# Gated group norm of a hybrid decoder layer: one 1/512 matrix spreads the means, GpSimd takes the root over all tokens

## The chip, the core and the metric

The kernel runs on one core of a Trainium2 chip. The metric is device time in microseconds (us), median of several runs. The engines are TensorE (PE in the rows; its weight loads are PEld), VectorE (DVE), ScalarE (ACT), GpSimd (POOL) and SyncE (SP), which issues the loads.

## The reference, cut to what matters

The layer has a Mamba-2 branch (SSD) and an attention branch, then a gated FFN. The change touches only the gated norm at the end of the SSD branch:

```python
# y: (1, 256 tokens, 4096 channels), 8 groups of 512 channels
y = y + d_skip[:, None] * xh
y = y.reshape(b, s, 8, 512) * silu(z).reshape(b, s, 8, 512)
y = y * rsqrt(mean(y * y, axis=-1, keepdims=True) + 1e-5)   # one mean per token and group
y = y.reshape(b, s, 4096) * ssm_norm_w
y_ssm = y @ w_ssm_out
```

The input projection that feeds it is `u @ w_in`, with u of 256 tokens by 2048 channels, in float32.

## The kernel before

Activations lie with channels on the 128 partitions and tokens along the free dimension. For one group of 512 channels `y` is thus a tile of 128 partitions by 4 blocks by 256 tokens, and the norm needs a sum over the 4 blocks and over the partitions, and then the same factor on every partition for each token.

Weights are streamed in units of 512 KB through four slots. For each unit ScalarE writes `hi`, the rounded half (`hi_of`, L466), VectorE writes `lo = raw - hi` (`lo_of`, L901, a subtraction of 128x1024 with both inputs in SBUF), and TensorE multiplies both halves with the activations (`columns`, L1485 with 512 columns and L1487 with 256, 8 pairs in a unit; `rows`, L1470 to L1472). A unit's products wait for its `lo` (semaphore `lo_ready`). `hi` of a unit waits until the products of the unit four before have used the slot.

Every engine's program is written out by hand in its own order. The projection of the SSD branch runs in 8 groups of 20 units (`group`), then 16 units of queries and gates (`X_UN`), then blocks of 8 units per attention head group (`Q_UN`). While the units of group g run, the SSD work and norm of group g-1 are done beside them, at fixed units: `ssd_side` on VectorE and ScalarE, `ssd_after` on TensorE. The norm of one group before the change, with its unit numbers in VectorE's order:

- unit 12: `ssd_skip` writes `y`; unit 13: `ssd_gate`; ScalarE then squares into `ysq`.
- unit 17: `ssd_sum` (L1157), one reduction over the 4 blocks into `ysum`.
- TensorE, after its unit 16: `mean_y` (L1690), for each half of the tokens one product with `ysum` as weights and one column of 1/512, so that the means lie with tokens on the partitions, 128x2.
- unit 19: `ssd_mean` (L1162) adds eps. GpSimd: `y_root` (L424), a power of -0.5 over 128x2.
- next group, unit 0: `ssd_spread` (L1166) copies the roots to `rb`, 128x256. TensorE, after its unit 0: `turn_root` (L1697) transposes `rb` so that each token's root lies on every partition of PSUM.
- next group, unit 3: `ssd_scale` (L1171), four operations that read `y` and the roots in PSUM.

The last group's norm does the same in the 16 units of `X_UN` and, for the scaling, at unit 3 of the first block of `Q_UN`. GpSimd's other work in that region is the copies of keys and values (L431, L434) and the scaling of queries (L440).

Of the kernel before, what the change touches and what calls it, by code (L numbers as in the profile page):

```python
# [105 lines left out]
def build(nc, x, params, w_in, w_ssm, w_attn, w_o, w_fi, w_fo, fnorm, out):  # L106
# [5 lines left out]
    with ExitStack() as ctx:  # L112
# [19 lines left out]
        inv_w, top = place("inv_w", [P, TT], top)  # L132
# [36 lines left out]
        ysum, a = place("ysum", [P, SEQ], a)  # L169
# [9 lines left out]
        ysq, a = place("ysq", [P, 4, SEQ], region + 80 * KB)  # L179
        ktok, a = place("ktok", [P, TT, KVH, 2, HD], region + 80 * KB)  # L180
# [73 lines left out]
        y_summed, y_meaned, y_mean_ready, y_rstd = sem("y_summed"), sem("y_meaned"), sem("y_mean_ready"), sem("y_rstd")  # L254
        y_spread, y_rt, y_kept = sem("y_spread"), sem("y_rt"), sem("y_kept")
# [127 lines left out]
        def _(po):  # L383
# [5 lines left out]
            po.memset(inv_w[:], 1.0 / GW)  # L389
# [56 lines left out]
            q_scaled_in(1, B, J_X + 1)  # L446
            with po.Fori(1, KVH) as h:
# [449 lines left out]
        def _(ve):  # L897
# [257 lines left out]
            def ssd_sum(k):  # L1155
                ve.wait_ge(y_squared, k + 1)
                ve.tensor_reduce(ysum[:, :, None], ysq[:].rearrange("p i n -> p n i"), op=ALU.add, axis=AX.X) \  # L1157
                    .then_inc(y_summed, 1)

            def ssd_mean(k):  # L1160
                ve.wait_ge(y_meaned, k + 1)
                ve.tensor_scalar(ssum[:], ps[:, M + 3, SEQ:SEQ + TT], EPS, None, ALU.add).then_inc(y_mean_ready, 1)  # L1162

            def ssd_spread(k):
                ve.wait_ge(y_rstd, k + 1)
                ve.tensor_copy(rb[:], rstd[:, :, None].to_broadcast([P, TT, P])).then_inc(y_spread, 1)  # L1166

            def ssd_scale(k):
                ve.wait_ge(y_rt, k + 1)
                for i in range(4):  # L1170
                    last = ve.scalar_tensor_tensor(out=acts[:, ds(k * 4 + i, 1), :].rearrange("p a n -> p (a n)"),  # L1171
                                                   in0=y[:, i, :], scalar=pcol("ssm_norm", k * 4 + i),
                                                   in1=ps[:, M + 3, 0:SEQ], op0=ALU.mult, op1=ALU.mult)
                last.then_inc(y_kept, 1)

            STEPS = dict(inputs=5, low=8, high=9, skip=12, gate=13, sum=17, mean=19)

            def ssd_side(k, u, at=STEPS, older=True):
# [19 lines left out]
                if u == at["mean"]:  # L1198
                    ssd_mean(k)
# [714 lines left out]
```

## Time and profile before

| what | value |
|---|---|
| median of 3 runs | 1923.75 us (1923.6 to 1923.87) |
| the profiled execution's own time | 1923.14 us |
| its span, first to last instruction | 1921.4 us |
| PE busy | 1910.4 us, 99% |
| DVE busy | 1308.0 us, 68% |
| ACT busy | 1083.7 us, 56% |
| POOL busy | 38.0 us, 2% |
| granted TensorE clock, mean | 0.999 |

The busy times are of one profiled execution. PE busy counts modelled ends of pipelined products, so what one product costs is read from the distance between starts. The median of the runs is 0.6 us above the profiled execution's own time.

### The profile page before, as it was taken

To read this page: it belongs to the slowest core of one execution; us is meant where nothing else is said; L and a number is where in the kernel's file an instruction comes from. 1 tells how busy PE (TensorE), PEld (TensorE's weight loads), DVE (VectorE), ACT (ScalarE), POOL (GpSimd) and SP (SyncE) were. 2 spreads that over 40 slices of the span, in tenths; PEclk is the share of its full clock that TensorE was granted. 3 is DMA by queue.
4 is the path that set the end of the run, shared out by engine and by line. 5 is a ranking of instruction groups with operands and counts; after the bars stand their busy time and mean duration, and the time that the engine had idled before them with its cause. 6 is when DMAs were issued, how large, how long until landed. Compare 5 with 4: busy or idle time off the path is not lost.

```text
span 1921.4 us, 28874 instructions
## 1 busy us (share of the span) xinstructions
PE 1910.4 (99%) x10205; PEld 1624.1 (85%) x10205; DVE 1308.0 (68%) x1634; ACT 1083.7 (56%) x1478; POOL 38.0 (2%) x79
## 2 busy tenths in 40 slices
PE   9999999999999999999999999999999999999998
PEld 7888888888888878888888888888888888888886
DVE  6787788777878874645544778666666766645444
ACT  6566765677657764444344445666666666534443
POOL 1000000000010100000000000000000000000000
PEclk9999999999999999999999999999999999999999
DMA  7666666656654446666666576666666666566564
GB/s 248 198 187 186 187 195 190 190 170 196 206 160 137 131 127 213 196 189 195 196 190 194 186 240 207 188 186 195 188 192 190 186 186 193 188 198 195 192 194 143
DMA packets 294902, 361.52 MB, mean 188 GB/s; under 512 B 13168, under 2 KB 218032, under 8 KB 293424
## 3 DMA queue, kind: packets, MB, share of 16 engines
q1 hardware_dynamic: 294832, 360.59, 61.2%
q8 instruction: 43, 0.70, 0.1%
q14 instruction: 27, 0.22, 0.0%
HBM read 358.38 MB, written 2.16 MB: 188 GB/s over the span
## 4 chain that ended last, share of the span: by engine, by line
PE 99%; issue 0%; DMA 0%; DVE 0%; ACT 0%; SPq 0%; POOLq 0%; POOL 0%; DVEq 0%; ACTq 0%
PE ps L1485 36%; PE ps L1487 18%; PE ps L1470 14%; PE ps L1471 14%; PE ps L1472 14%; PE ps L1683 1%; PE ps L1611 1%; PE ps L1624 1%; PE ps L1635 0%; PE ps L1684 0%; PE ps L1672 0%; PE ps L1527 0%; PE ps L1562 0%; PE ps L1636 0%; PE ps L1668 0%
## 5 line engine op out<-in xcount | busy, mean ns | idle before, releaser
L901 DVE TENSOR_TENSOR lo<-raw,hi 128x1024 fp32r<-128x1024 f32 x652 | 796.2, 1227 | 467.6 <-ACT hi L466 461.6
L1485 PE MATMUL ps<-uHL,hi 128*128 128x512 f32 x2944 | 1035.3, 396 | 0.0
L466 ACT ACTIVATE hi<-raw 128x1024 fp32r<-128x1024 f32 x652 | 682.8, 1055 | 511.3 <-PE ps L1472 379.7
L1487 PE MATMUL ps<-uHL,lo 128*128 128x256 f32 x2944 | 823.9, 280 | 0.0
L1485 PEld LDWEIGHTS ps<-uHL,hi 128*128 128x128 f32 x2944 | 551.7, 187 | 130.5 <-issue 5.4
L1487 PEld LDWEIGHTS ps<-uHL,lo 128*128 128x128 f32 x2944 | 555.9, 189 | 0.0
L1472 PE MATMUL ps<-hi,aL 128*128 128x512 f32 x384 | 149.5, 389 | 0.0
L1472 PE MATMUL ps<-hi,hL 128*128 128x512 f32 x352 | 136.9, 389 | 0.0
L1471 PE MATMUL ps<-lo,hH 128*128 128x512 f32 x352 | 136.9, 389 | 0.0
L1470 PE MATMUL ps<-hi,hH 128*128 128x512 f32 x352 | 136.9, 389 | 0.0
L476 ACT ACTIVATE hb<-ps 128x512 f32<-128x512 f32 x92 | 54.8, 595 | 121.5 <-PE ps L1487 121.5
L1470 PE MATMUL ps<-hi,uHL 128*128 128x512 f32 x288 | 113.5, 394 | 0.9 <-DVE lo L908 0.9
L1472 PE MATMUL ps<-hi,uHL 128*128 128x512 f32 x288 | 112.2, 390 | 0.0
L1471 PE MATMUL ps<-lo,uHL 128*128 128x512 f32 x288 | 112.2, 389 | 0.0
L1470 PE MATMUL ps<-hi,aHs 128*128 128x512 f32 x256 | 100.9, 394 | 0.0
L1471 PE MATMUL ps<-lo,aHs 128*128 128x512 f32 x256 | 99.7, 389 | 0.0
L1472 PEld LDWEIGHTS ps<-hi,aL 128*128 128x128 f32 x384 | 72.1, 188 | 15.1
L1470 PEld LDWEIGHTS ps<-hi,hH 128*128 128x128 f32 x352 | 66.1, 188 | 13.8
L1471 PEld LDWEIGHTS ps<-lo,hH 128*128 128x128 f32 x352 | 66.1, 188 | 13.8
L1472 PEld LDWEIGHTS ps<-hi,hL 128*128 128x128 f32 x352 | 66.1, 188 | 13.5
L1092 DVE SCALAR_TENSOR_TENSOR cv<-cs,par,cv 128x253 f32<-128x253 f32 (+1 forms) x144 | 63.3, 481 | 14.2 <-ACT cv L580 7.0
L1470 PEld LDWEIGHTS ps<-hi,uHL 128*128 128x128 f32 x288 | 54.1, 188 | 12.1 <-DVE lo L908 1.1
(204 smaller groups left out, 1695.3 us busy)
## 6 DMA issues: line engine op xcount, KB each, us to landing
raw<-w_in SPq DMA_DIRECT2D x261, 512.0 KB, 4.2
raw<-w_ffn_in SPq DMA_DIRECT2D x176, 512.0 KB, 3.8
raw<-w_ffn_out SPq DMA_DIRECT2D x88, 512.0 KB, 4.4
raw<-w_ssm_out SPq DMA_DIRECT2D x64, 512.0 KB, 4.2
raw<-w_attn_out SPq DMA_DIRECT2D x32, 512.0 KB, 4.4
raw<-w_o SPq DMA_DIRECT2D x32, 512.0 KB, 4.5
rows_b<-cum_rows SPq DMA_DIRECT2D x8, 1024.0 KB, 6.7
x_tok<-x SPq DMA_DIRECT2D x8, 256.0 KB, 5.4
```

Of the source, the lines that this page charges most:

```text
L466: act.activation(hi[:, s % SLOTS, :], raw[:, s % SLOTS, :], ACT.Copy).then_inc(hi_ready, 1)
L476: act.activation(hb[:], ps[:, pair:pair + 2, SEQ:2 * SEQ], ACT.Copy).then_inc(half_kept, 1)
L901: ve.tensor_tensor(lo[:, s % SLOTS, :], raw[:, s % SLOTS, :], hi[:, s % SLOTS, :].bitcast(F32), ALU.subtract).then_inc(lo_ready, 1)
L1092: last = ve.scalar_tensor_tensor(out=cv[:, slot, sh:SEQ], in0=cs[:, i, 0:SEQ - sh], scalar=pcol("conv_w", ch * TAPS + tap), in1=cv[:, slot ...
L1470: pe.matmul(out, w[0], x[0], start=start, stop=False)
L1471: pe.matmul(out, w[0], x[1], start=False, stop=False)
L1472: return pe.matmul(out, w[1], x[0], start=False, stop=stop)
L1485: pe.matmul(ps[:, pair + c, :], w_hi, uHL[:, kk].rearrange("p a n -> p (a n)"), start=kk == 0, stop=False)
L1487: last = pe.matmul(ps[:, pair + c, 0:SEQ], w_lo, uHL[:, kk, 0, :], start=False, stop=kk == k - 1)
L1611: last = pe.matmul(ps[:, M + j, cols], qT[r, i, blk * P:(blk + 1) * P], kcur[r, keys], start=True, stop=True)
L1624: last = pe.transpose(ps[:, M + 2 + o // 512, o % 512:o % 512 + P], lg[:, i, j, c * P:(c + 1) * P], ident[:])
L1683: pe.matmul(out, xd[:, 0, c], dec[:, h, 0:2, :].rearrange("p c n -> p (c n)"), start=True, stop=False)
```

## The change

The sum over the four blocks is made by two additions (128x512, 128x256). The sum is then split into a rounded half `ymH` and a rest `ymL`, and TensorE multiplies a full 128x128 matrix of 1/512 (`mean_w`) with each, 256 columns, both into the same PSUM region. Every partition then has the mean of every token. VectorE adds eps and writes all of it to SBUF (`y_rt`, 128x256), GpSimd takes the power in place over 128x256, and `ssd_scale` reads `y_rt` at unit 10 instead of 3 (last group: unit 7 instead of 3). `ssd_spread` and `turn_root` are gone. The last group's root stands behind the first copies and query scalings on GpSimd. The first transposes of attention probabilities wait for `y_mean_ready` instead of `y_kept`.

```diff
@@ gpsimd
-            po.memset(inv_w[:], 1.0 / GW)
+            po.memset(mean_w[:].bitcast(F32), 1.0 / GW)
@@
             def y_root(k):
                 po.wait_ge(y_mean_ready, k + 1)
-                po.tensor_tensor(rstd[:], ssum[:], neghalf[:], ALU.pow).then_inc(y_rstd, 1)
-
-            with po.Fori(0, G) as g:
+                po.tensor_tensor(y_rt[:], y_rt[:], neghalf[:, 0:1].to_broadcast([P, SEQ]), ALU.pow).then_inc(y_rooted, 1)
+
+            with po.Fori(0, G - 1) as g:
                 y_root(g)
@@
             q_scaled_in(0, A, J_X + 1)
             q_scaled_in(1, B, J_X + 1)
+            y_root(G - 1)
@@ vector
             def ssd_sum(k):
                 ve.wait_ge(y_squared, k + 1)
-                ve.tensor_reduce(ysum[:, :, None], ysq[:].rearrange("p i n -> p n i"), op=ALU.add, axis=AX.X) \
-                    .then_inc(y_summed, 1)
-
-            def ssd_mean(k):
+                ve.tensor_tensor(ysq[:, 0:2, :], ysq[:, 0:2, :], ysq[:, 2:4, :], ALU.add)
+                ve.drain()
+                ve.tensor_tensor(ysq[:, 2, :], ysq[:, 0, :], ysq[:, 1, :], ALU.add)
+                ve.drain()
+                ve.tensor_copy(ymH[:], ysq[:, 2, :])
+                ve.drain()
+                ve.tensor_tensor(ymL[:], ysq[:, 2, :], ymH[:].bitcast(F32), ALU.subtract).then_inc(y_summed, 1)
+
+            def ssd_root(k):
                 ve.wait_ge(y_meaned, k + 1)
-                ve.tensor_scalar(ssum[:], ps[:, M + 3, SEQ:SEQ + TT], EPS, None, ALU.add).then_inc(y_mean_ready, 1)
-
-            def ssd_spread(k):
-                ve.wait_ge(y_rstd, k + 1)
-                ve.tensor_copy(rb[:], rstd[:, :, None].to_broadcast([P, TT, P])).then_inc(y_spread, 1)
+                ve.tensor_scalar(y_rt[:], ps[:, M + 3, 0:SEQ], EPS, None, ALU.add).then_inc(y_mean_ready, 1)
 
             def ssd_scale(k):
-                ve.wait_ge(y_rt, k + 1)
+                ve.wait_ge(y_rooted, k + 1)
@@
-                                                   in1=ps[:, M + 3, 0:SEQ], op0=ALU.mult, op1=ALU.mult)
+                                                   in1=y_rt[:], op0=ALU.mult, op1=ALU.mult)
@@
-            STEPS = dict(inputs=5, low=8, high=9, skip=12, gate=13, sum=17, mean=19)
+            STEPS = dict(scale=10, inputs=5, low=8, high=9, skip=12, gate=13, sum=17, mean=19)
@@
-            LAST_STEPS = dict(inputs=5, low=7, high=8, skip=11, gate=12, sum=13, mean=15)
+            LAST_STEPS = dict(scale=9, inputs=5, low=7, high=8, skip=11, gate=12, sum=13, mean=15)
@@
-                if u == 3:
+                if u == 7:
                     ssd_scale(G - 1)
@@ tensor
-                    pe.wait_ge(y_kept, G)
+                    pe.wait_ge(y_mean_ready, G)
@@
             def mean_y(k):
                 pe.wait_ge(y_summed, k + 1)
-                for t in range(TT):
-                    last = pe.matmul(ps[:, M + 3, SEQ + t:SEQ + t + 1], ysum[:, t * P:(t + 1) * P], inv_w[:, 0:1],
-                                     start=True, stop=True)
-                last.then_inc(y_meaned, 1)
-
-            def turn_root(k):
-                pe.wait_ge(y_spread, k + 1)
-                for t in range(TT):
-                    last = pe.transpose(ps[:, M + 3, t * P:(t + 1) * P], rb[:, t, :], ident[:])
-                last.then_inc(y_rt, 1)
+                pe.matmul(ps[:, M + 3, 0:SEQ], mean_w[:], ymH[:], start=True, stop=False)
+                pe.matmul(ps[:, M + 3, 0:SEQ], mean_w[:], ymL[:], start=False, stop=True).then_inc(y_meaned, 1)
```

How the change moves VectorE's instructions is seen at the end of one group and the start of the next (the branch at L1203, in the new code L1206, is the loop's head; `lo` is the subtraction of a unit). Before:

```order
L901 TENSOR_TENSOR lo<-raw,hi 128x1024 [waits hi_ready] x2
L1157 TENSOR_REDUCE ysum<-ysq 128x256 [waits y_squared]
L901 TENSOR_TENSOR lo<-raw,hi 128x1024 [waits hi_ready]
L951 TENSOR_TENSOR szb<-ps,hb 128x512 [waits second_half_kept]
L957 TENSOR_TENSOR szb<-szb,rt 128x512
L901 TENSOR_TENSOR lo<-raw,hi 128x1024 [waits hi_ready]
L1162 TENSOR_SCALAR ssum<-ps 128x2 [waits y_meaned]
L1203 UNCONDITIONAL_BRANCH
L1203 ISA
L901 TENSOR_TENSOR lo<-raw,hi 128x1024 [waits hi_ready]
L1165 REGISTER_ALU
L1166 COPY rb<-rstd 128x256 [waits y_rstd]
```

After, at the same place:

```order
L1160 TENSOR_TENSOR ysq<-ysq 128x512 [waits y_squared]
L1162 TENSOR_TENSOR ysq<-ysq 128x256
L1164 CAST ymH<-ysq 128x256
L1166 TENSOR_TENSOR ymL<-ysq,ymH 128x256
L904 TENSOR_TENSOR lo<-raw,hi 128x1024 [waits hi_ready]
L954 TENSOR_TENSOR szb<-ps,hb 128x512 [waits second_half_kept]
L960 TENSOR_TENSOR szb<-szb,rt 128x512
L904 TENSOR_TENSOR lo<-raw,hi 128x1024 [waits hi_ready]
L1170 TENSOR_SCALAR y_rt<-ps 128x256 [waits y_meaned]
L1206 UNCONDITIONAL_BRANCH
L1206 ISA
L904 TENSOR_TENSOR lo<-raw,hi 128x1024 [waits hi_ready]
```

One reduction has become four operations, the addition of eps covers 256 columns, and the copy that waited for GpSimd's root is gone. Directly behind the addition the `lo` of the next unit follows, in both.

GpSimd's queue from the loop over the groups to the loop over the head groups, before:

```order
L424 TENSOR_TENSOR rstd<-ssum,neghalf 128x2 [waits y_mean_ready]
L426 REGISTER_ALU
L426 COMPARE_AND_BRANCH
L431 COPY kcur<-kdup 128x256 [waits kdup_ready]
L434 COPY vcur<-vtok 128x128
L440 TENSOR_TENSOR qT<-qT,rt 128x512 [waits pair_a_free]
L440 TENSOR_TENSOR qT<-qT,rt 128x512 [waits pair_b_free]
```

After:

```order
L426 TENSOR_TENSOR y_rt<-y_rt,neghalf 128x256 [waits y_mean_ready]
L428 REGISTER_ALU
L428 COMPARE_AND_BRANCH
L433 COPY kcur<-kdup 128x256 [waits kdup_ready]
L436 COPY vcur<-vtok 128x128
L442 TENSOR_TENSOR qT<-qT,rt 128x512 [waits pair_a_free]
L442 TENSOR_TENSOR qT<-qT,rt 128x512 [waits pair_b_free]
L426 TENSOR_TENSOR y_rt<-y_rt,neghalf 128x256 [waits y_mean_ready]
```

The power now has 256 columns instead of 2, and the last of the eight stands behind the copies and the two query scalings.

## Rows read from the trace of the kernel before

**Rows 1.** The page: chain of work that ended last, by engine.

```profile
PE 99%; issue 0%; DMA 0%; DVE 0%; ACT 0%; SPq 0%; POOLq 0%; POOL 0%; DVEq 0%; ACTq 0%
```

**Rows 2.** Timeline of PE around the mean's products: start us, us, what.

```profile
147.40 0.39 PE L1485 MATMUL ps<-uHL,hi 128*128 128x512 f32 x1
...
147.75 0.40 PE L1485 MATMUL ps<-uHL,hi 128*128 128x512 f32 x1
...
148.10 0.50 PE L1690 MATMUL ps<-inv_w,ysum 128*128 128x1 f32 x4
...
148.89 0.40 PE L1485 MATMUL ps<-uHL,hi 128*128 128x512 f32 x1
```

**Rows 3.** Timeline of PE around the transposed roots.

```profile
159.29 0.40 PE L1485 MATMUL ps<-uHL,hi 128*128 128x512 f32 x1
...
159.64 0.38 PE L1697 MATMUL ps<-ident,rb 128*128 128x128 f32 x2
...
160.21 0.40 PE L1485 MATMUL ps<-uHL,hi 128*128 128x512 f32 x1
```

**Rows 4.** Timeline of DVE from the first group's mean to its scaling.

```profile
149.45 0.15 DVE L1162 TENSOR_SCALAR ssum<-ps 128x2 f32<-128x2 f32 x1
149.52 1.22 DVE L901 TENSOR_TENSOR lo<-raw,hi 128x1024 fp32r<-128x1024 f32 x1
...
152.68 1.22 DVE L901 TENSOR_TENSOR lo<-raw,hi 128x1024 fp32r<-128x1024 f32 x1 [1.06 <-ACT hi L466]
...
162.59 1.65 DVE L1171 SCALAR_TENSOR_TENSOR acts<-y,par,ps 128x256 f32 x4
```

**Rows 5.** DVE's operations for the sum: forms, count, busy us, mean ns.

```profile
L1157 DVE TENSOR_REDUCE ysum<-ysq 128x256 f32<-128x1024 f32 x8 | 16.1, 2009 | 0.0
...
L957 DVE TENSOR_TENSOR szb<-szb,rt 128x512 f32<-128x512 f32 x16 | 11.1, 693 | 1.5
```

**Rows 6.** Timelines of DVE and PE in the second group: `lo` of unit 16, mean.

```profile
203.63 1.22 DVE L901 TENSOR_TENSOR lo<-raw,hi 128x1024 fp32r<-128x1024 f32 x1 [0.16 <-issue]
...
209.60 0.50 PE L1690 MATMUL ps<-inv_w,ysum 128*128 128x1 f32 x4
```

**Rows 7.** Timeline of POOL: first and last root of the loop.

```profile
149.68 1.61 POOL L424 TENSOR_TENSOR rstd<-ssum,neghalf 128x2 f32<-128x2 f32 x1 [119.04 <-DVE ssum L1162]
...
568.92 0.69 POOL L424 TENSOR_TENSOR rstd<-ssum,neghalf 128x2 f32<-128x2 f32 x1 [49.10 <-DVE ssum L1162]
```

**Rows 8.** POOL's other powers and multiplication (the last: min/median/max ns).

```profile
L417 POOL TENSOR_TENSOR rstd<-ssum,neghalf 128x2 f32<-128x2 f32 x2 | 1.4, 706 | 533.8 <-DVE ssum L914 533.8
L417 POOL TENSOR_TENSOR rstd<-ssum,neghalf 128x1 f32<-128x1 f32 x2 | 1.1, 551 | 724.0 <-DVE ssum L914 724.0
...
L440 POOL TENSOR_TENSOR qT<-qT,rt x8: 1288/1294/2261, 570.2 to 673.4; 128x512 f32<-128x512 f32 x8
```

**Rows 9.** Timelines of DVE and POOL where both have work, short windows.

```profile
570.02 1.30 DVE L901 TENSOR_TENSOR lo<-raw,hi 128x1024 fp32r<-128x1024 f32 x1
570.22 2.26 POOL L440 TENSOR_TENSOR qT<-qT,rt 128x512 f32<-128x512 f32 x1
...
571.25 2.31 DVE L901 TENSOR_TENSOR lo<-raw,hi 128x1024 fp32r<-128x1024 f32 x1
```

**Rows 10.** Timelines at the last group's root: DVE's mean, PE's next work.

```profile
568.68 0.16 DVE L1162 TENSOR_SCALAR ssum<-ps 128x2 f32<-128x2 f32 x1 [3.40 <-PE ps L1690]
...
574.09 0.38 PE L1697 MATMUL ps<-ident,rb 128*128 128x128 f32 x2
574.40 0.93 PE L1611 MATMUL ps<-kcur,qT 64*128 64x128 f32 x8
```

**Rows 11.** PE's start; a window behind its last product (end: clock, DMA share, GB/s).

```profile
1.64 3.04 PE L1549 MATMUL ps<-ident 128*128 128x128 f32 x13 [1.64 <-POOL ident L386]
...
6.13 0.82 PE L1549 MATMUL ps<-ident 128*128 128x128 f32 x6
...
1918.00:1921.40 3.40, 0.00 (x0) 0.00 (x0) 0.00 (x0) 0.00 (x0) 0.00 (x0) 0.50 0.69 284
```

More of the change, by code:

```diff
@@ L131, in build @@
         neghalf, top = place("neghalf", [P, TT], top)
-        inv_w, top = place("inv_w", [P, TT], top)
         ss, top = place("ss", [P, TT, 4], top)
@@ L168, in build @@
         cbm, a = place("cbm", [P, 3, P], a)
-        ysum, a = place("ysum", [P, SEQ], a)
+        mean_w, a = place("mean_w", [P, P], a, F32R)
+        y_rt, a = place("y_rt", [P, SEQ], a)
         act_rows, a = place("act_rows", [SH, SEQ], a)
@@ L179, in build @@
         ysq, a = place("ysq", [P, 4, SEQ], region + 80 * KB)
+        ymH, b = place("ymH", [P, SEQ], a, F32R)
+        ymL, b = place("ymL", [P, SEQ], b, F32R)
         ktok, a = place("ktok", [P, TT, KVH, 2, HD], region + 80 * KB)
@@ L253, in build @@
         y_done, y_skipped, y_gated, y_squared = sem("y_done"), sem("y_skipped"), sem("y_gated"), sem("y_squared")
-        y_summed, y_meaned, y_mean_ready, y_rstd = sem("y_summed"), sem("y_meaned"), sem("y_mean_ready"), sem("y_rstd")
-        y_spread, y_rt, y_kept = sem("y_spread"), sem("y_rt"), sem("y_kept")
+        y_summed, y_meaned, y_mean_ready = sem("y_summed"), sem("y_meaned"), sem("y_mean_ready")
+        y_rooted, y_kept = sem("y_rooted"), sem("y_kept")
         ah_ready, al_ready = sem("ah_ready"), sem("al_ready")
@@ L1172, in ssd_scale @@
                                                    in0=y[:, i, :], scalar=pcol("ssm_norm", k * 4 + i),
-                                                   in1=ps[:, M + 3, 0:SEQ], op0=ALU.mult, op1=ALU.mult)
+                                                   in1=y_rt[:], op0=ALU.mult, op1=ALU.mult)
                 last.then_inc(y_kept, 1)
-            STEPS = dict(inputs=5, low=8, high=9, skip=12, gate=13, sum=17, mean=19)
+            STEPS = dict(scale=10, inputs=5, low=8, high=9, skip=12, gate=13, sum=17, mean=19)
             def ssd_side(k, u, at=STEPS, older=True):
-                if u == 0 and older:
-                    ssd_spread(k - 1)
-                if u == 3 and older:
+                if u == at["scale"] and older:
                     ssd_scale(k - 1)
@@ L1191, in ssd_side @@
                 if u == at["skip"]:
+                    ve.drain()
                     ssd_skip(k)
@@ L1198, in ssd_side @@
                 if u == at["mean"]:
-                    ssd_mean(k)
+                    ssd_root(k)
             group(0, 0, 0, dt_side)
@@ L1217, in _ @@
                     halves(qT[:, 2:4, :], B, H_X + 2)
-            ssd_spread(G - 1)
             def q_first(h, u):
@@ L1688, in mean_y @@
                 pe.wait_ge(y_summed, k + 1)
-                for t in range(TT):
-                    last = pe.matmul(ps[:, M + 3, SEQ + t:SEQ + t + 1], ysum[:, t * P:(t + 1) * P], inv_w[:, 0:1],
-                                     start=True, stop=True)
-                last.then_inc(y_meaned, 1)
-            def turn_root(k):
-                pe.wait_ge(y_spread, k + 1)
-                for t in range(TT):
-                    last = pe.transpose(ps[:, M + 3, t * P:(t + 1) * P], rb[:, t, :], ident[:])
-                last.then_inc(y_rt, 1)
+                pe.matmul(ps[:, M + 3, 0:SEQ], mean_w[:], ymH[:], start=True, stop=False)
+                pe.matmul(ps[:, M + 3, 0:SEQ], mean_w[:], ymL[:], start=False, stop=True).then_inc(y_meaned, 1)
             def ssd_after(k, u, older=True, at=(2, 9, 16)):
-                if u == 0 and older:
-                    turn_root(k - 1)
                 if u == at[0]:
@@ L1756, in _ @@
                 ssd_after(G - 1, u, at=(2, 8, 13))
-                if u == X_UN - 1:
-                    turn_root(G - 1)
             for u in range(Q_UN):
```

## The prediction

> **What bounds the kernel now.** I read the page's chain of work first: 99% of the span is TensorE's own work, one product after another [rows 1]. So a term counts if it takes time out of TensorE's row, puts time into it, or makes it wait, and everything else is free as long as it stays hidden. Next I read TensorE's timeline where the norm's small products stand [rows 2, 3], to get from distances between starts what they cost. Then I read VectorE and GpSimd side by side, because the norm passes through both, and VectorE also makes the `lo` half that each unit's products wait for [rows 4, 7, 9]. The reader should see there how far `lo` runs ahead of TensorE and what happens when both engines want to work at once.
>
> **TensorE's own work: about 3.4 us less.** A pair L1485/L1487 takes 0.35 us from start to start (147.40 to 147.75). From 147.75 to 148.89 there are two pairs and the mean's products: 1.14 - 0.70 = 0.44 us for `mean_y` [rows 2]. From 159.29 to 160.21 there are two pairs and the transposes: 0.92 - 0.70 = 0.22 us for `turn_root` [rows 3]. Eight of each: 8 x 0.66 = 5.3 us removed. Added are two products of 256 columns. A pair has 768 columns in 0.35 us, so 256 columns are 0.117 us; two are 0.23 us, times 8 is 1.9 us. Net -3.4 us. If the two together cost as much as the products that they replace, 0.44 us, it is -1.8 us.
>
> **VectorE's own work: nothing.** The reduction of 2.0 us goes [rows 5]. In its place come additions of 512 and 256 columns (0.69 us for 512 [rows 5], at most that for 256), a cast and a subtraction of 256 columns and three drains; 1.7 to 2.6 us together, so the sum is ready 0.3 us earlier to 0.6 us later. The addition of eps grows from 0.15 us [rows 4] to something under the 0.69 us of 512 columns, I take 0.35; the copy to `rb` goes. The scaling, 1.65 us [rows 4], moves from unit 3 to unit 10, in front of a dense stretch. There `lo` of unit 16 starts at 203.63 and ends 204.85; TensorE reaches the mean's products behind unit 16 at 209.60, and a unit is 8 pairs, 2.8 us, so it started unit 16 at 206.8 [rows 2, 6]. The lead at its smallest is 2.0 us against 1.65 us moved: covered. Without that cover it would cost at most 8 x 1.65 = 13 us, and VectorE has idle time to make it up: at 152.68 it waited 1.06 us for `hi` [rows 4].
>
> **GpSimd's power over 256 columns: this decides.** The trace has no power of 256 columns. It has 551 ns for one column and 706 ns (mean) for two [rows 8], and 0.69 us for two where nothing disturbed the root of the loop [rows 7]. The multiplication of 512 columns takes 1.29 us [rows 8]. So from below: at the multiplication's rate, at most 2.5 ns a column, 256 columns cost about 0.64 us over the 0.55 us of one, D = 1.2 us. From above: 0.55 + 255 x 0.17 (0.72 - 0.55, the slower two-column root behind the mean of 706) = 44 us. The two powers are the nearest rows, the same operation on the same engine, and their difference cannot be explained by a rate of 2.5 ns. I take 0.14 us a column: D = 0.55 + 255 x 0.14 = 36 us. A long loop can be cheaper per column than its first two; I keep the whole range for that.
>
> **Who waits during D.** At 570 us both engines have work [rows 9]. VectorE's `lo` starts at 570.02 and ends 571.3; GpSimd's multiplication starts at 570.22 and takes 2.26 us instead of 1.29, so it got going when `lo` ended, and ended at 572.48. VectorE's next `lo` started at 571.25 and took 2.31 us instead of 1.22: it waited until 572.4. The two took turns, an instruction at a time. The first root of the loop shows the same: `lo` from 149.52 to 150.74, the power from 149.68 takes 1.61 us instead of 0.69 and ends 0.55 us behind that `lo` [rows 4, 7]. The trace shows it with instructions of about 1 us; whether a power that mostly computes keeps VectorE out for 36 us it does not show. I take it that it does.
> The Trainium skill ("SBUF — State Buffer", section on practical consequences) says that a VectorE instruction with two SBUF inputs contends with a GpSimd instruction that reads SBUF, and that the first to issue has the shared pair for the whole instruction while the other fully blocks. By that rule the power blocks each `lo` for all of D; were it wrong for a computing instruction, the next part would be zero.
>
> **The wait, group by group.** Behind the addition of eps VectorE goes straight into `lo` of the next group's unit 0, as now, and holds off GpSimd until 150.74 + 0.2 = 150.9 [rows 4]. The power runs until 150.9 + D. The next `lo`, unit 1, now at 152.68 [rows 4], is held, and with it everything behind it in VectorE's queue. It ends at 150.9 + D + 1.2 = 152.1 + D. TensorE, which does `turn_root` behind unit 0 at 159.64 [rows 3], needs unit 1 there, 0.2 us earlier by the cheaper mean: 159.4. It stands still for D - 7.3 us. With D = 36 that is 28.7 us, seven times: 201 us. ScalarE's `hi` halves and the loads of three more units are done meanwhile, so a `lo` of 1.2 us stands against 2.8 us of products and VectorE regains its lead; I add nothing for that. The scaling at unit 10 then comes long after the root and waits for nothing.
> The last group: VectorE stands waiting for the means at 568.68 [rows 10], the power starts before the next `lo` of 570.02 [rows 9], at about 569.0, and that `lo` ends at 570.2 + D. TensorE needs it behind the scores, 574.40 + 0.93 less 0.4 us for the removed and cheaper products: 574.9 [rows 10]. Wait D - 4.7 = 31.3 us.
> Together 232 us.
>
> **The clock after each stop.** After the last product the granted clock stands at 0.50, the 1.2 GHz level [rows 11]. At the program's start 13 transposes take 3.04 us, 0.234 each, and six later ones 0.82 us, 0.137 each [rows 11]; so work after a stop loses about 13 x 0.097 = 1.3 us. Eight stops: 10 us, from 0 to twice that.
>
> **Sum.** -3.4 + 232 + 10 = 238.6 us on the profiled execution's own 1923.1 us. The median of the runs is 0.6 us above that one: 1923.75 + 238.6 = 2162 us.
>
> **The rivals.**
> (a) *Held, but cheaper per column.* If the rate falls in a long instruction, D lies between 7.3 and 28 us. At 0.07 us a column D = 18.4 us: stops of 7 x 11.1 + 13.7 = 91 us, with 10 for the clock and -3.4: 2022 us. For it: two columns say little of 256. Against: the second column cost 0.14 us, no sign of overlap.
> (b) *The power is short.* Below D = 7.3 us, 27 ns a column, the loop's stops vanish; at the 1.2 us of the lower bound even `lo` hardly notices. Time 1923.75 - 3.4 = 1920.4 us. Against it: the second column's 0.14 us.
> The Trainium skill ("GPSIMD Engine Reference", section "Elementwise — side-by-side cycle accounting") gives about 2.6 cycles an element for a two-input operation; the estimate by that page is 256 x 2.6 / 1.2 GHz = 0.55 us and thus this case. The multiplication's row agrees with it (1.29 us for 512 columns), the power's rows do not.
> (c) *The power does not keep VectorE out* while it computes. Then D = 36 us ends at 149.9 + 36 = 186. A unit of a group takes (209.60 - 148.10) / 20 = 3.07 us [rows 2, 6], so VectorE has unit 10's `lo` at 152.7 + 9 x 3.07 + 1.2 = 181.5 and after two operations of 0.7 us stands at the scaling, at 183: it waits 3 us, about its lead. The time is 1920.4 us, not slower, and from D = 36 on each further us costs up to 8. For it: the power reads and writes little per us. Against: the turns of [rows 9] are whole instructions.
> (d) *Dearer* than 44 us: above 2225 us.
>
> **How the numbers follow.** A measurement of this kernel tells about 0.2% (4 us) from no change. Chances: forecast (D from 28 to 44, 2095 to 2225 us) 0.50; (a) 0.31, 1924 to 2095 us; (b) 0.08; (c) 0.08; (d) 0.03. In (b) and (c) the gain of at most 3.4 us lies just inside 0.2%: mostly same. So faster 0.06, same 0.12, slower 0.82. The range has to leave out (b), (c) and a little of (a): 1980 us is a D of about 13 us. At the top, D = 44 us gives 2225, and 2230 with more lost to the clock. The likeliest case's own range is 2095 to 2230.
>
> **What would show it.** In the trace after: eight powers of tens of us each on GpSimd, ending one `lo` before TensorE goes on; one `lo` per group of about D minus 1 us, recorded as long or as idle time of VectorE; eight stops of TensorE behind a unit 0, and a granted clock of 0.50 in them; no stop elsewhere; two products of 256 columns per group 0.23 us apart from their neighbours. The prediction is wrong if `lo` subtractions of 1.2 us lie inside a power (then (c)), or if the power's row reads below 7 us (then (b)). Wrong in size alone if the row is between.

## The result, and the profile after

| | before | changed |
|---|---|---|
| median of the runs (us) | 1923.61 | 2013.62 |
| lowest and highest | 1923.02, 1923.87 | 2012.22, 2015.17 |
| span of the profiled execution | 1921.4 | 2012.0 |
| ratio, 95% interval | | 1.0467 [1.0456, 1.0479] |

The change costs 90 us, 4.7%. I had forecast 238.6. The time lies in the range of 1980 to 2230 us, but below the likeliest case's own 2095, and the way there is not the forecast one. That it lies in the range is luck: the part between 1980 and 2095 stood there for rival (a), a power cheaper than forecast, and the power turned out dearer.

The page of the changed kernel, chain of work by engine and then the group of the power:

```profile
PE 66%; issue 29%; POOL 5%; DVE 0%; POOLq 0%; ACT 0%; DVEq 0%; ACTq 0%
...
L426 POOL TENSOR_TENSOR y_rt<-y_rt,neghalf 128x256 f32<-128x256 f32 x8 | 336.2, 42031 | 295.4 <-DVE y_rt L1170 295.4
```

In [rows 1] the chain was 99% TensorE. Now it is 66%, and POOL is in it. The 29% of "issue" are time for which the page names no cause: in the chain they are mostly six pieces of 69 us, one from each power of the loop to the next, so the chain alone does not say what happens there. The power takes 42.03 us. Against the one-column power of [rows 8] that is (42.03 - 0.55) / 255 = 0.163 us a column; the forecast had 0.14 and 36 us, with 44 as its upper bound. The forecast said that such a power keeps VectorE out. VectorE's timeline of the changed kernel, from the addition of eps to the scaling:

```profile
149.92 0.42 DVE L1170 TENSOR_SCALAR y_rt<-ps 128x256 f32<-128x256 f32 x1
150.26 1.22 DVE L904 TENSOR_TENSOR lo<-raw,hi 128x1024 fp32r<-128x1024 f32 x1
...
152.64 1.23 DVE L904 TENSOR_TENSOR lo<-raw,hi 128x1024 fp32r<-128x1024 f32 x1 [1.17 <-ACT hi L469]
...
155.93 1.23 DVE L904 TENSOR_TENSOR lo<-raw,hi 128x1024 fp32r<-128x1024 f32 x1 [2.07 <-ACT hi L469]
...
183.59 1.22 DVE L904 TENSOR_TENSOR lo<-raw,hi 128x1024 fp32r<-128x1024 f32 x1
...
185.51 0.69 DVE L960 TENSOR_TENSOR cs<-cs,rt 128x512 f32<-128x512 f32 x1
...
192.76 1.67 DVE L1175 SCALAR_TENSOR_TENSOR acts<-y,par,y_rt 128x256 f32 x4 [6.56 <-POOL y_rt L426]
194.35 1.22 DVE L904 TENSOR_TENSOR lo<-raw,hi 128x1024 fp32r<-128x1024 f32 x1
```

The same stretch: all `lo` subtractions from the power's start to its end (min/median/max ns, first and last start), and GpSimd's powers of groups 1, 2, 7 and 8:

```profile
L904 DVE TENSOR_TENSOR lo<-raw,hi x11: 1215/1225/1227, 150.3 to 183.6; 128x1024 fp32r<-128x1024 f32 x11
```

```profile
150.42 42.05 POOL L426 TENSOR_TENSOR y_rt<-y_rt,neghalf 128x256 f32<-128x256 f32 x1 [119.91 <-DVE y_rt L1170]
219.81 42.03 POOL L426 TENSOR_TENSOR y_rt<-y_rt,neghalf 128x256 f32<-128x256 f32 x1 [27.33 <-DVE y_rt L1170]
...
566.24 42.03 POOL L426 TENSOR_TENSOR y_rt<-y_rt,neghalf 128x256 f32<-128x256 f32 x1 [27.22 <-DVE y_rt L1170]
626.96 42.03 POOL L426 TENSOR_TENSOR y_rt<-y_rt,neghalf 128x256 f32<-128x256 f32 x1 [11.84 <-DVE y_rt L1170]
```

Eleven subtractions with two SBUF inputs stand in the stretch of one power (the first starts 0.16 us before it, the other ten inside it), the slowest 1.227 us, against 1.22 in [rows 4]. None is kept out. VectorE does all it has up to unit 10 and then waits for the power at the scaling. What is queued behind the scaling, `lo` first, is late for TensorE. TensorE's stops of more than a few us in total, by what they waited for (us in total, times, longest), and last the one wait of ScalarE that is taken up under the end of the block:

```profile
PE ps L1487 <- DVE lo L904: 30.5, 12, 4.9
...
PE ps L1626 <- ACT acts L553: 21.6, 1, 21.6
...
PE ps L1472 <- DVE lo L904: 8.4, 1, 8.4
...
ACT acts L553 <- DVE acts L1175: 23.1, 1, 23.1
```

TensorE's 60.5 us are not the 90. So I cut the span by landmarks: starts of the first and seventh power, of the first scores, of the first merge (VectorE's `mraw`), of the FFN convolution (ScalarE's `gv`, first and last of its passes). Before, then changed; the source views of two of the landmarks:

```profile
L1257 DVE TENSOR_TENSOR mraw<-ps,sgs x4: 1225/1225/1225, 726.9 to 1053.3; 128x1024 f32<-128x1024 f32 x4
...
L828 ACT ACTIVATE gv<-gs,par x44: 583/596/604, 1199.1 to 1665.9; 128x256 f32<-128x256 f32 x44
```

```profile
L1259 DVE TENSOR_TENSOR mraw<-ps,sgs x4: 1224/1224/1224, 807.9 to 1134.3; 128x1024 f32<-128x1024 f32 x4
...
L831 ACT ACTIVATE gv<-gs,par x44: 585/596/605, 1280.1 to 1755.9; 128x256 f32<-128x256 f32 x44
```

| stretch (us) | before | changed | more |
|---|---|---|---|
| power 1 to power 7 | 368.5 | 415.8 | 47.3 |
| power 7 to first scores | 56.2 | 65.6 | 9.4 |
| first scores to first merge | 152.5 | 176.1 | 23.6 |
| first merge to FFN convolution | 472.2 | 472.2 | 0 |
| FFN convolution, first to last `gv` | 466.8 | 475.8 | 9.0 |

That is 89.3 of the 90.6 us; the rest is 0.7 ahead of the first power and 0.6 behind the last `gv`. Four amounts at four places, and the last of them at a place that the change does not touch.

### The profile page after: what moved, and what is told of

The parts are those of the page before. It is cut to its first block, busy times and chain, and to the rows that moved or that the text cites. A ratio compares the mean times of both kernels' runs of the same rounds, so it can differ in the third digit from the quotient of the medians.

```text
span 2012.0 us, 28849 instructions
## 1 busy us (share of the span) xinstructions
PE 1940.2 (96%) x10173; PEld 1636.1 (81%) x10173; DVE 1308.5 (65%) x1650; ACT 1082.0 (54%) x1478; POOL 360.4 (18%) x79
## 4 chain that ended last, share of the span: by engine, by line
PE 66%; issue 29%; POOL 5%; DVE 0%; POOLq 0%; ACT 0%; DVEq 0%; ACTq 0%
PE ps L1487 18%; PE ps L1472 12%; PE ps L1474 12%; PE ps L1473 12%; PE ps L1489 9%; POOL y_rt L426 4%; PE ps L1613 1%; PE ps L1626 1%; PE ps L1637 0%; DVE acts L1175 0%; PE ps L1638 0%; POOL qT L442 0%; DVE lo L904 0%; POOL nslope L395 0%; POOL rstd L419 0%
## 5 line engine op out<-in xcount | busy, mean ns | idle before, releaser
L1487 PE MATMUL ps<-uHL,hi 128*128 128x512 f32 x2944 | 1058.7, 403 | 30.7 <-DVE lo L904 30.5
L1487 PEld LDWEIGHTS ps<-uHL,hi 128*128 128x128 f32 x2944 | 559.6, 190 | 176.2 <-DVE lo L904 35.8
L1489 PEld LDWEIGHTS ps<-uHL,lo 128*128 128x128 f32 x2944 | 562.5, 191 | 0.0
L426 POOL TENSOR_TENSOR y_rt<-y_rt,neghalf 128x256 f32<-128x256 f32 x8 | 336.2, 42031 | 295.4 <-DVE y_rt L1170 295.4
```

Of the source, the lines that this page charges most:

```text
L426: po.tensor_tensor(y_rt[:], y_rt[:], neghalf[:, 0:1].to_broadcast([P, SEQ]), ALU.pow).then_inc(y_rooted, 1)
L1487: pe.matmul(ps[:, pair + c, :], w_hi, uHL[:, kk].rearrange("p a n -> p (a n)"), start=kk == 0, stop=False)
L1489: last = pe.matmul(ps[:, pair + c, 0:SEQ], w_lo, uHL[:, kk, 0, :], start=False, stop=kk == k - 1)
```

## The experiments

Each is an edit of the changed kernel unless said otherwise. e1, e2, e6, e8 and f3 leave out the scale of some tokens: they are there for their times only. The runs of the kernel before beside them had medians of 1923.5 to 1923.6 us.

| label | edit | median (us) | ratio [95%] |
|---|---|---|---|
| e1_pow128 | power over 128 columns | 1938.92 | 1.0079 [1.0063, 1.0096] |
| e2_pow2 | power over 2 columns | 1938.45 | 1.0078 [1.0061, 1.0094] |
| e3_scale12 | scaling at unit 12 | 1981.23 | 1.0300 [1.0283, 1.0317] |
| e4_scale3 | scaling at unit 3 | 2135.59 | 1.1103 [1.1085, 1.1122] |
| e5_actroot | root on ScalarE | 1949.31 | 1.0133 [1.0116, 1.0150] |
| e6_both | power over 2 columns, then a streaming and a computing instruction | 1938.59 | 1.0077 [1.0061, 1.0094] |
| e7_filled | transposes in the stops | 2014.76 | 1.0473 [1.0456, 1.0491] |
| e8_last2 | last power over 2 columns | 1996.99 | 1.0384 [1.0367, 1.0401] |
| f1_before_less32 | kernel before, six tiles 32 bytes lower | 1932.72 | 1.0049 [1.0035, 1.0063] |
| f2_spare | changed, the six tiles 32 bytes higher | 2004.40 | 1.0419 [1.0402, 1.0435] |
| f3_pow2_spare_last3 | e2, tiles as in f2, last scaling at unit 3 | 1923.26 | 0.9999 [0.9990, 1.0008] |
| f4_actroot3 | e5, reciprocal at unit 1, scalings at unit 3 | 1922.33 | 0.9994 [0.9985, 1.0004] |

**How much of it is the power's length.**

```diff
-                po.tensor_tensor(y_rt[:], y_rt[:], neghalf[:, 0:1].to_broadcast([P, SEQ]), ALU.pow).then_inc(y_rooted, 1)
+                po.tensor_tensor(y_rt[:, 0:P], y_rt[:, 0:P], neghalf[:, 0:1].to_broadcast([P, P]), ALU.pow).then_inc(y_rooted, 1)   # e1
+                po.tensor_tensor(y_rt[:, 0:TT], y_rt[:, 0:TT], neghalf[:, 0:1].to_broadcast([P, TT]), ALU.pow).then_inc(y_rooted, 1)  # e2
```

> The changed kernel with the power over 128 of the 256 columns (the scale of the other tokens is left out). Theory, the loss is VectorE's wait in order at the scaling of unit 10: the power takes 0.16 us a column, 21 us, ends long before unit 10, and all stops go: 1920.4 us, 3.4 less than before. Rival, the power keeps the lo subtractions out while it runs: 8 x (21 - 7.3) more, about 2030 us, more than the changed kernel itself would allow, so at least most of the 90 us loss stays in proportion.

> The changed kernel with the power over 2 columns only (the scale of nearly all tokens is left out): what is left of the change is the sum in four operations, the two products with the full matrix, no transposes, and the later scaling. Theory: 1920.4 us, 3.4 us less than before, and equal to the kernel with 128 columns. Rival, the four operations, the denser VectorE stretch around unit 10 or the later scaling cost part of the 90 us: above 1924 us.

With 128 columns the power takes 21.63 us:

```profile
L426 POOL TENSOR_TENSOR y_rt<-y_rt,neghalf 128x128 f32<-128x128 f32 x8 | 173.1, 21632 | 373.7 <-DVE y_rt L1170 373.7
```

With 2 columns it takes 1.6 (e2), with 256 it takes 42.03. The last 128 columns cost (42.03 - 21.63) / 128 = 0.159 us each, the 126 before them (21.63 - 1.61) / 126 = 0.159 as well: no fall of the rate such as the rival (a) had. These rows hold some 0.9 us that is not the power's own: it is issued beside a `lo` and starts behind it, as in [rows 4, 7], where 2 columns took 1.61 us beside a `lo` and 0.69 without. The first power of e7, issued 0.2 us ahead of the `lo`, took 41.14 us, and that `lo` 1.49 instead of 1.22. Powers of 21.6 us and of 1.6 us give the same time, so a power that ends before unit 10 costs nothing, and 75 us of the 90 are the power's length beyond that. The other 15 remained in both kernels, so both forecasts of 1920.4 us were missed by 18.

**Does GpSimd keep VectorE out?** Behind each power of 2 columns in the loop, e6 puts a multiplication that streams 2520 columns and then a power of 40 columns, both on a scratch tile.

```diff
+                if not isinstance(k, int):
+                    po.drain()
+                    po.tensor_tensor(scr[:, 0:2520], scr[:, 0:2520], scr[:, 0:2520], ALU.mult).then_inc(scr_done, 1)
+                    po.tensor_tensor(scr[:, 2520:2560], scr[:, 2520:2560], neghalf[:, 0:1].to_broadcast([P, 40]), ALU.pow).then_inc(scr_done, 1)
```

> The kernel with the power over 2 columns (scale of nearly all tokens left out), and behind each of the seven roots in the loop GpSimd does two more things on scratch columns: a multiplication of 2520 columns (6.3 us) and then a power of 40 columns (7 us). Theory, only an instruction that streams keeps VectorE's two-input instructions out: a lo that comes during the multiplication is held until its end, and those during the power run in 1.22 us; the holds are shorter than the lead, so the time is 1920 to 1928 us. Rival A, whole-instruction lock whatever the instruction: lo is held during the power too. Rival B, no lock at all beyond a slower rate: lo runs at 1.22 to 2 us during the multiplication too.

GpSimd's timeline in e6 around the first of them, and VectorE's of the same time:

```profile
150.38 1.61 POOL L429 TENSOR_TENSOR y_rt<-y_rt,neghalf 128x2 f32<-128x2 f32 x1 [119.56 <-DVE y_rt L1177]
152.15 4.39 POOL L432 TENSOR_TENSOR scr<-scr 128x2520 f32<-128x2520 f32 x1 [0.16 <-issue]
156.50 7.72 POOL L433 TENSOR_TENSOR scr<-scr,neghalf 128x40 f32<-128x40 f32 x1
```

```profile
150.21 1.22 DVE L911 TENSOR_TENSOR lo<-raw,hi 128x1024 fp32r<-128x1024 f32 x1
...
152.68 6.13 DVE L911 TENSOR_TENSOR lo<-raw,hi 128x1024 fp32r<-128x1024 f32 x2 [1.25 <-ACT hi L476]
...
161.23 2.36 DVE L911 TENSOR_TENSOR lo<-raw,hi 128x1024 fp32r<-128x1024 f32 x2 [1.03 <-ACT hi L476]
```

```profile
L911 DVE TENSOR_TENSOR lo<-raw,hi x6: 1216/1226/4935, 150.2 to 164.1; 128x1024 fp32r<-128x1024 f32 x6
```

The `lo` that starts at 152.68 falls into the multiplication and takes 4.94 us, until 157.6, about one `lo` of 1.22 beyond the multiplication's end at 156.5. The next starts at about 157.6 inside the power and takes 6.13 - 4.94 = 1.19 us; the pair at 161.23 is also undisturbed. In the other six groups the `lo` that comes during the multiplication takes 3.26 to 3.42 us and ends 1.1 behind it each time. So the multiplication keeps VectorE out until its end, and the powers do not. The turns of [rows 9] held for the first kind. I call the two kinds streaming and computing by their price, 1.7 ns a column against 159; which property of the power leaves VectorE its inputs was not tried apart. The time is that of e2 (1938.59 against 1938.45 us): the holds are covered by the lead of `lo`. The forecast of 1920 to 1928 us was missed because of the 15 us that e2 has too, not because of the holds. The 40-column power's 7.72 us hold 1.1 of the delayed `lo`, behind which it started.

The Trainium skill ("SBUF — State Buffer", section "Who interferes with whom") says that a VectorE instruction with two SBUF inputs contends with any GpSimd instruction that reads SBUF. The multiplication agrees with it (4.94 us against 1.22), the `lo` inside a power do not (1.227 at most), and here the measurement decides.

**Where the waiter stands.** The scaling is moved alone.

```diff
-            STEPS = dict(scale=10, inputs=5, low=8, high=9, skip=12, gate=13, sum=17, mean=19)
+            STEPS = dict(scale=12, inputs=5, low=8, high=9, skip=12, gate=13, sum=17, mean=19)   # e3
+            STEPS = dict(scale=3, inputs=5, low=8, high=9, skip=12, gate=13, sum=17, mean=19)    # e4
```

> The changed kernel with the scaling of the seven loop groups at unit 12 instead of 10, directly ahead of the skip that writes y again. Theory: VectorE does the lo of units 11 and 12 and a convolution (5.5 us) before it waits, of the 6.6 us wait about 1 is left, TensorE never stops in the groups and keeps its full clock: the seven groups give back 7 x 7.7 = 54 us, 1958 us, with the last group's loss of about 36 us left. Rival, the loss in the groups comes from the port or from the power's length as such, whatever waits for it: about 2013 us as the changed kernel.

> The changed kernel with the scaling of the loop groups back at unit 3. Theory: VectorE stands behind the lo of unit 3 from 162.4 until the power ends at 192.5; TensorE has halves up to unit 3 until 168 and gets unit 4 at 195.3: a stop of 27 us and 3 us of half clock behind it, 7 x 30 = 210 us on 1920.4 + 36: about 2165 us. Rival, the position does not matter because the loss has another cause: about 2013 us.

One power of each, e3 and then e4 (in brackets the idle time from the power's end to the next one's start):

```profile
214.31 42.03 POOL L426 TENSOR_TENSOR y_rt<-y_rt,neghalf 128x256 f32<-128x256 f32 x1 [21.94 <-DVE y_rt L1170]
```

```profile
240.40 42.03 POOL L426 TENSOR_TENSOR y_rt<-y_rt,neghalf 128x256 f32<-128x256 f32 x1 [47.62 <-DVE y_rt L1170]
```

A group's period is the power plus what VectorE does from the scaling to the next addition of eps: 42.03 + 47.6 = 89.6 us with the scaling at unit 3, 42.03 + 27.3 = 69.3 at unit 10, 42.03 + 21.9 = 63.9 at unit 12. Before it was 368.5 / 6 = 61.4, TensorE's own. So the order of VectorE's queue closes a loop: power, scaling, all units behind it, sum, mean, next power. Each unit that the scaling stands later takes 2.7 to 2.9 us off the period until TensorE's own work is longer: (89.6 - 69.3) / 7 = 2.9 and (69.3 - 63.9) / 2 = 2.7. That VectorE sets the period is seen in its waits from 192 to 220 us of the changed kernel: 6.6 us for the power, 1.4 us in short gaps without a named cause, 0.4 us for ScalarE and none for TensorE. The forecasts had the direction and missed the size: 1958 us for e3, where the period stays 2.5 us above TensorE's, and 2165 us for e4. The periods give it: 6 x (63.9 - 69.3) = -32 and 6 x (89.6 - 69.3) = 122 us, and the medians differ from the changed kernel's by -32.4 and 122.0.

**Is it the clock?** TensorE's timeline of the changed kernel behind the first scaling, then windows there (us, busy us with count of PE, PEld, DVE, ACT and POOL, granted clock, DMA share, GB/s):

```profile
191.59 0.28 PE L1489 MATMUL ps<-uHL,lo 128*128 128x256 f32 x1
195.62 0.80 PE L1487 MATMUL ps<-uHL,hi 128*128 128x512 f32 x1 [3.76 <-DVE lo L904]
...
196.43 0.63 PE L1487 MATMUL ps<-uHL,hi 128*128 128x512 f32 x1
```

```profile
195.00:202.00 7.00, 6.38 (x21) 5.47 (x22) 6.12 (x13) 0.85 (x2) 0.00 (x0) 0.53 0.72 233
202.00:220.00 18.00, 17.82 (x102) 15.19 (x102) 16.71 (x24) 10.27 (x18) 0.19 (x1) 1.00 0.70 198
```

After a stop of 3.76 us the pairs stand 0.64 us apart instead of 0.35, at a granted clock of 0.53 over seven us, nearly all at the 1.2 GHz level. That is about 3 us of TensorE's work. Over the next four groups, in stretches of 70 us from 260 to 540, the granted clock is 0.95 to 0.98, so 1.4 to 3.5 us a group. So in e7 the stop is filled with transposes that nobody reads (28 behind unit 10 of each loop group):

```diff
+                if u == 10 and at[2] == 16:
+                    for _ in range(28):
+                        pe.transpose(ps[:, M + 3, SEQ:SEQ + P], ident[:], ident[:])
```

> The changed kernel with 28 idle transposes (0.13 us each, 3.7 us) on TensorE behind unit 10 of each group, where it would otherwise stop for 3.8 us and more. They write a part of PSUM that nobody reads then. Theory, a good third of the loss is the half clock behind each stop (9 pairs of 0.64 us instead of 0.35): the clock stays at 1.00 in the seven groups, and 7 x 2.7 = 19 us come back: about 1995 us. Rival, the clock follows something else, or the products behind the stop are slow for want of lo halves: no gain, 2013 us or more.

The windows of e7, its wait for `lo` and its second power:

```profile
193.00:196.00 3.00, 3.00 (x30) 2.58 (x27) 0.34 (x1) 1.72 (x2) 2.37 (x1) 1.00 0.05 14
196.00:200.00 4.00, 4.00 (x34) 3.83 (x33) 3.82 (x9) 1.06 (x1) 0.00 (x0) 1.00 0.09 16
200.00:210.00 10.00, 10.00 (x61) 8.74 (x59) 9.21 (x14) 1.65 (x3) 0.00 (x0) 1.00 0.81 266
```

```profile
PE ps L1487 <- DVE lo L904: 21.4, 20, 2.2
```

```profile
222.70 42.03 POOL L426 TENSOR_TENSOR y_rt<-y_rt,neghalf 128x256 f32<-128x256 f32 x1 [27.33 <-DVE y_rt L1170]
```

The clock stays at 1.00, here and in all stretches of 70 us from 190 to 540, and the time does not change: 2014.76 against 2013.62 us, where 1995 was forecast. The gap from power to power is 27.33 us, to the digit that of the changed kernel. The explanation by the clock falls for the seven groups. The low clock was there, but it ran beside VectorE's catching up, which sets the period; what TensorE lost at the low clock it otherwise spends in short waits for `lo`: the transposes filled 7 x 3.7 = 26 us, and yet the waits fell only from 30.5 to 21.4.

**The end of the block.** In e8 only the last power has 2 columns.

```diff
+                n = TT if isinstance(k, int) else SEQ    # k is a number for the last group only
...
```

> The changed kernel with the last group's power over 2 columns (the scale of that group's tokens is left out); the seven others have all 256. Theory: the last group alone costs 21.6 us of waiting for the attention output that stands behind the scaling on ScalarE, 8 us for lo and 6 us of half clock, 36 us: 1977 us. Rival, the seventh stop only moves to the next wait in the attention blocks: little gain, over 2000 us.

It gains 16.6 us of the 36 forecast, 16.3 of them between the first scores and the first merge (176.1 to 159.8), and the stretch before the scores nearly none (64.5 against 65.6). So the 9.4 us there are the seventh power's: the scaling at unit 9 makes `lo` late, 8.4 us in the wait row above. The eighth power costs the attention block 16. The chain there, in the changed kernel, VectorE and then TensorE:

```profile
669.03 2.67 DVE L1175 SCALAR_TENSOR_TENSOR acts<-y,par,y_rt 128x256 f32<-128x256 f32 x4 [15.63 <-POOL y_rt L426]
```

```profile
672.25 1.51 PE L1626 MATMUL ps<-ident,lg 128*128 128x128 f32 x6 [21.61 <-ACT acts L553]
```

The eighth power starts at 626.96 and ends at 668.99; VectorE stood at the scaling 15.6 us, and ScalarE waits at unit 7 for `y_kept`, the scaling's signal, 23.1 us (the last wait row above). TensorE waits for ScalarE's probabilities, queued behind that wait. The forecast had VectorE alone in view. With the short power there is still a stop, in e2:

```profile
PE ps L1626 <- ACT acts L553: 4.9, 1, 4.9
```

Here ScalarE reaches its unit 7 before VectorE has scaled in its own unit 7. So this part belongs to the place of the scaling, not to the power: 7.3 us with the lower clock behind it (159.8 against 152.5).

**The 9 us in the FFN.** Its products take 353.3 ns a pair in the changed kernel and 346.7 before, 21 passes over. Its instructions are the same; what differs is that the new tiles moved the six behind them (`ss`, `ssum`, `rstd`, `rstd1`, `rb`, `rt`), which TensorE does not read there, by 32 bytes. The granted clock is 1.00 there in both. f1 is the kernel before with `inv_w` placed elsewhere, so that those six lie 32 bytes lower; f2 is the changed kernel with a spare tile ahead of them.

```diff
-        inv_w, top = place("inv_w", [P, TT], top)
+        inv_w, _ = place("inv_w", [P, TT], region + 122 * KB)          # f1, in the kernel before
+        spare, top = place("spare", [P, TT], top)                      # f2, in the changed kernel
```

> The kernel before with nothing changed but the place of the tile inv_w in SBUF: it goes behind the other tiles, so the six tiles placed after it (ss, ssum, rstd, rstd1, rb, rt) lie 32 bytes lower, as in the changed kernel. All runs of the changed kind without a 32-byte tile there took 353.3 ns for a pair of FFN products (475.8 us for 21 passes of that loop), before and the one run with such a tile 346.7 ns (466.8 us). Theory, the place alone makes this: pairs of 353 ns in the FFN loop and 1933 us, 9 over before. Rival, it hangs on the program's code, of which this kernel keeps all: 346.7 ns and 1923.6 us.

> The changed kernel with an unused 32-byte tile where inv_w stood, nothing else. Theory, the place of the tiles behind it costs 9 us in the FFN loop: 2004 us. Rival, it is the changed code: 2013.6 us as the changed kernel.

The FFN's passes in f1 and in f2:

```profile
L828 ACT ACTIVATE gv<-gs,par x44: 585/596/605, 1199.5 to 1675.2; 128x256 f32<-128x256 f32 x44
```

```profile
L832 ACT ACTIVATE gv<-gs,par x44: 587/596/605, 1281.5 to 1748.4; 128x256 f32<-128x256 f32 x44
```

475.7 us for the kernel before with the tiles moved, 466.9 for the changed one with the tiles moved back, and the medians move by 9 as forecast, to 1932.72 and 2004.40. The 9 us go with the placement in both directions. The other stretches of the table change by under 2 us in f1 and f2; the first power comes 2.0 to 2.1 us later in both, whichever way the tiles moved. Which of the six it is, and by what mechanism, stays open.

**The root elsewhere.** e5 takes GpSimd out: ScalarE takes the square root straight from PSUM with eps as its bias at its unit 0, VectorE a reciprocal ahead of the scaling.

```diff
+                act.activation(y_rt[:], ps[:, M + 3, 0:SEQ], ACT.Sqrt, bias=epsc[:, 0:1]).then_inc(y_mean_ready, 1)
...
+                ve.reciprocal(y_rt[:], y_rt[:])
```

> The changed kernel with the root taken elsewhere: ScalarE takes a square root of the means plus eps straight from PSUM (behind its unit 0 of the next group) and VectorE a reciprocal of 256 columns ahead of the scaling at unit 10; GpSimd has no part in it. Theory: ScalarE needs a table load each way (2.6 us a group) and 0.4 us, both hidden under its idle time; VectorE's reciprocal of 256 columns under 2 us is hidden too; all stops go and TensorE keeps the 3.4 us of saved products: 1920.4 us, 0.18% under before. Rival, the table loads and the reciprocal make lo or hi late: above 1924 us.

The rival happened: 1949.31 us. Here the FFN takes 466.7 us (its constant of eps has the size of the spare tile), the attention block 162.1 against 152.5. The other 18 us are ahead of the scores, which start at 592.8 instead of 574.4: with the reciprocal of 1.75 us and the scaling in front of VectorE's dense stretch, TensorE waits for `lo`, 13.3 us of them (the other 5 are not split further):

```profile
PE ps L1491 <- DVE lo L911: 13.3, 16, 1.6
...
PE ps L1630 <- ACT acts L551: 6.7, 1, 6.7
```

f4 is e5 with the reciprocal at unit 1 and all scalings at unit 3, where VectorE has room. It does the whole norm, as the changed kernel does. f3 is e2 with the spare tile and the last scaling at unit 3; its other scalings stay at 10.

> The changed kernel with the power over 2 columns (the scale of nearly all tokens is left out), the 32-byte tile kept, and the last scaling back at unit 3. With 2 columns 1938.5 us were left, 18 over the 1920.4 of my sum. Theory: 9 of them are the place of the tiles and 8 the stop at the attention block (4.9 us, and 3.4 of half clock), which the last scaling at unit 7 makes because ScalarE's unit 7 waits for it: both go, 1920.4 to 1922 us. Rival, one of the two is not the cause: about 1930 us.

> The root by ScalarE (square root from PSUM plus eps) and VectorE (reciprocal of 256 columns, 1.75 us, at unit 1), the scaling at unit 3 in all groups, the 32-byte tile's place taken by a constant. With the reciprocal and scaling at unit 10 this took 1949.3 us: 13 us of waits for lo, in pieces up to 1.6 us, and 6.7 at the attention block. Theory: those waits come from 3.4 us more of VectorE in its dense stretch and go at units 1 and 3, where it idles: 1920.4 to 1924 us. Rival, ScalarE's two table loads a group (2.6 us) are what is late: waits stay, above 1930 us.

Both are the kernel before again: 0.9999 [0.9990, 1.0008] and 0.9994 [0.9985, 1.0004]. f3 has no loss left, and no gain: 1923.26 us where 1920.4 to 1922 was forecast. f4, at 1922.33, lies in its forecast of 1920.4 to 1924; ScalarE's table load (one more a group, 1.28 us) is not what was late. So the 15 us that e2 still lost are 9 of placement and 7 of the last scaling's place, less about 1. And the saving of 3.4 us is missing. TensorE's timeline of f3 at the second mean, VectorE's last operation before it, and f3's wait row and source row for the mean's first product:

```profile
209.55 0.40 PE L1488 MATMUL ps<-uHL,hi 128*128 128x512 f32 x1
...
210.08 0.39 PE L1692 MATMUL ps<-ymH,mean_w 128*128 128x256 f32 x1
210.30 0.28 PE L1693 MATMUL ps<-ymL,mean_w 128*128 128x256 f32 x1
210.42 0.40 PE L1488 MATMUL ps<-uHL,hi 128*128 128x512 f32 x1
```

```profile
209.60 0.43 DVE L1167 TENSOR_TENSOR ymL<-ysq,ymH 128x256 fp32r<-128x256 f32 x1
```

```profile
PEld ps L1692 <- DVE ymL L1167: 1.5, 4, 0.4
...
L1692 PE MATMUL ps<-ymH,mean_w x8: 278/372/389, 149.0 to 568.5; 128*128 128x256 f32 x8
```

From pair to pair it is 210.42 - 209.55 = 0.87 us with one pair of 0.35 in it: this mean costs 0.52 us, not 0.23. Its first product starts 0.05 us after VectorE's `ymL` is done, at 210.03. Four of the eight means wait so, 1.5 us together; the first of all, which does not, costs 0.24. That leaves 5.3 - 1.9 - 1.5 = 1.9 us of saving. f4, with its scalings at unit 3, waits as well (four means, 1.4 us), so the later scaling is not what makes the sum late there; what does is open. From the first mean to the first scores it is 574.3 - 149.0 = 425.3 us against 574.40 - 148.10 = 426.3 [rows 2, 10], 1.0 less; f3 reaches the first mean 0.9 us later, which says little, as f1, with the instructions of the kernel before, reaches its first power 2.1 us later. All of this is less than the comparison can tell.

## Why the prediction was right or wrong

1. **TensorE's own work, -3.4 us: mis-sized.** I counted the products by their columns. In f3 it is -1.0 to -1.9 us, since the sum arrives too late for half of the means. A mean that does not wait costs what I counted, 0.24 against 0.23. My other bound, -1.8, was nearer, but for another reason.
2. **VectorE's own work, nothing: held for `lo`.** It did not hold for the sum, whose lateness is in item 1. f3 has the scalings at unit 10 in all groups but the last and loses nothing. That the cover is as thin as the 2.0 us against 1.65 say is seen in e5: another 1.75 us of reciprocal at the same place, and TensorE waits for `lo` 16 times.
3. **The power's price, 36 us within 1.2 to 44: right in kind.** 42.03 us, 0.163 us a column where 0.14 was taken. Reading the difference between two rows of one and two columns as a rate was the right choice over the multiplication's 2.5 ns.
4. **Who waits during D: this step failed.** "I take it that it does" was the decision that a computing power keeps VectorE out. Eleven `lo` at 1.22 us inside one power, and e6's pair of instructions, show that it does not. So the 7 x 28.7 us behind unit 0 do not exist, and the rival (c) is what happened: its mechanism and its place (the scaling at unit 10). Its 1920.4 us did not come, since D was 42.03 and not 36. VectorE's part of the period is 27.3 us, so TensorE's 61.4 leave room for a power of 34.1 (an estimate from these two), and 42.03 - 34.1 = 7.9 us in each of six periods are the 47.3 us. Its rule of up to 8 us for each us beyond 36 would give 1920.4 + 48 = 1968; the last group and the placement are what is above that. I had put a chance of 0.08 on it, because the trace of before shows only instructions that stream.
5. **The last group, 31.3 us: about right in sum by luck, wrong in way.** It was forecast as a `lo` that the eighth power holds off. It came as 33.0 us: 9.4 us (seventh power, scaling at unit 9) and 23.6 us in the attention block, of which 7.3 are the scaling's place and 16 the eighth power. "No stop elsewhere" was wrong: ScalarE's wait for `y_kept` at its unit 7 did not stand in my list of who waits for the moved step.
6. **The clock, 10 us: present, not on the path.** The low clock stood behind the stops, 1.4 to 3.5 us of TensorE's work a group, against the 1.3 that I had read from the program's start. Filling the stops in seven groups brought it to 1.00 and changed nothing in the time (e7), since VectorE's loop sets the period. At the last stop, where TensorE is waited for, the time after it may count; this was not tried apart.
7. **Not in the sum at all: the placement of six tiles, 9.0 us.** f1 and f2 show it both ways.

The measured parts together: 47.3 + 9.4 + 23.6 + 9.0 = 89.3 of 90.6 us.

## What to carry to other kernels

When an instruction grows long on one engine, do not take it for granted that it keeps its neighbours out as a short streaming one did: measure which of them it holds; then follow the loop that its result closes through the other engines' queues, for its length is that of the iteration as soon as it exceeds TensorE's. List every engine that waits on the moved step's signal, not only the one that executes it. And before explaining a difference of half a per cent by the edit, look at a stretch that the edit does not touch: if that changed too, compare at equal placement.

## What the runs showed of the hardware

- GpSimd's power costs 0.16 us a column of 128 partitions (0.55 us for 1, 21.63 for 128, 42.03 for 256, the last two with some 0.9 us behind a `lo`), while its multiplication of 2520 columns took 4.39 us, 1.7 ns a column. The price of these two functions there differs by a factor of some ninety. The Trainium skill ("GPSIMD Engine Reference", section "Elementwise — side-by-side cycle accounting") gives some 2.6 cycles an element of a two-input operation. With that page's clock of 1.2 GHz, as an estimate, the multiplication's 1.74 ns are 2.1 cycles and the power's 159 ns some 190: it does not hold for the power.
- During such a power VectorE's two-input subtractions ran at 1.215 to 1.227 us; during the multiplication one took 4.94 us.
- Six small tiles 32 bytes higher or lower, which TensorE does not read, change its pair of products in the FFN from 346.7 to 353.3 ns and the whole by 9 us, 0.5%. The stretch from the first merge to the FFN convolution took 472.2 us either way. The cause is open.
